# Order of the recurrence's level work and the weight splits in one segment of a transformer kernel

## The reference

```python
u = rmsnorm(h, attn_norm_w)
q, f_raw, i_in, g_out, b_gate, c_gate, x_conv, gate_a, gate_b = split(u @ w_in)
q = silu(q); f = lb + (1 - lb) * sigmoid(f_raw); logf = log(f); k = 1 - f; v = i_in
# per head, in chunks, G = cumsum(logf):
A[t, s] = sum(q[t] * k[s] * exp(G[t] - G[s]))   for s <= t
o = (q * exp(G)) @ S + A @ v                     # S: state from the chunks before
y_b = b_gate * causal_dwconv(c_gate * x_conv, conv_w)      # three taps
merged = sigmoid(gate_a) * rmsnorm(o) * silu(g_out) + sigmoid(gate_b) * y_b
```

## Time and profile before

| | |
|---|---|
| median of 3 runs | 1200.52 us (1199.38 to 1200.52) |
| the profiled execution | 1200.52 us, its span 1198.7 us |
| TensorE busy | 1149.8 us, 96% |
| VectorE busy | 878.9 us, 73% |
| ScalarE busy | 616.6 us, 51% |
| "conv" on TensorE | 784.4 to 883.9 us |

### The profile page before, as it was taken

How to read it: one execution, slowest core, us unless ns; L and a number is a source line. 1 busy time by engine, 2 the same in 40 slices (tenths; PEclk the granted TensorE clock), 3 DMA queues, 4 the chain that set the end, 5 groups by cost and what they waited for, 6 DMA issues and landing times.

```text
span 1198.7 us, 22749 instructions
## 1 busy us (share of the span) xinstructions
PE 1149.8 (96%) x8630; PEld 1088.2 (91%) x8630; DVE 878.9 (73%) x1486; ACT 616.6 (51%) x989; POOL 70.6 (6%) x134
## 2 busy tenths in 40 slices
PE   4999989999999999899999999999999999999997
PEld 4898679999888898799998889999999999999997
DVE  5799788998887985696554577787764766777643
ACT  4547546444336566654443465544443646555532
POOL 0101110211111310000000000000000000000000
PEclk9899989999999999999999999999999999999999
DMA  9947656999874743476455334433333453555531
GB/s 365 413 167 264 237 202 221 367 394 356 291 300 141 248 157 120 155 281 219 175 179 206 141 121 148 156 139 107 141 141 106 164 187 111 207 180 192 188 141 36
DMA packets 43131, 241.67 MB, mean 202 GB/s; under 512 B 5152, under 2 KB 7584, under 8 KB 20400
## 3 DMA queue, kind: packets, MB, share of 16 engines
q1 hardware_dynamic: 28912, 191.29, 44.3%
q0 software_dynamic: 14144, 49.37, 11.6%
HBM read 237.48 MB, written 1.06 MB: 199 GB/s over the span
## 4 chain that ended last, share of the span: by engine, by line
PE 82%; DVE 8%; ACT 5%; issue 3%; DMA 1%; SPq 0%; POOL 0%; DVEq 0%; ACTq 0%; POOLq 0%
PE acc L1914 20%; PE acc L1915 19%; PE acc L1916 19%; PE aux L2024 3%; PE aux L2026 3%; PE aux L2025 3%; PE aux L2401 2%; DVE wlo L1043 2%; ACT whi L583 1%; DMA x<-xT 1%; PE aux L1916 1%; PE aux L1914 1%; PE aux L1915 1%; ACT free_hlo L628 1%; PE aux L2055 1%
## 5 line engine op out<-in xcount | busy, mean ns | idle before, releaser
L1914 PE MATMUL acc<-hhi,whi 128*128 128x256 f32 (+3 forms) x1976 | 567.2, 287 | 6.8 <-DVE hlo L1064 4.0
L1915 PE MATMUL acc<-hlo,whi 128*128 128x256 f32 (+3 forms) x1976 | 560.2, 283 | 0.0
L1916 PE MATMUL acc<-hhi,wlo 128*128 128x256 f32 (+3 forms) x1976 | 557.7, 282 | 0.0
L1043 DVE TENSOR_TENSOR wlo<-raw,whi 128x1024 fp32r<-128x1024 f32 x338 | 412.8, 1223 | 178.6 <-ACT whi L583 178.1
L583 ACT ACTIVATE whi<-raw 128x1024 fp32r<-128x1024 f32 x338 | 357.1, 1057 | 189.7 <-PE acc L1916 119.4
L1914 PEld LDWEIGHTS acc<-hhi,whi 128*128 128x128 f32 x1976 | 374.0, 189 | 12.0 <-DVE hlo L1064 6.2
L1916 PEld LDWEIGHTS acc<-hhi,wlo 128*128 128x128 f32 x1976 | 375.7, 190 | 0.0
L1915 PEld LDWEIGHTS acc<-hlo,whi 128*128 128x128 f32 x1976 | 374.5, 190 | 0.2
L1072 DVE CUSTOM_DVE_ANT_0 lev<-lev,vec 128x1024 f32<-128x1024 f32 x56 | 71.7, 1280 | 1.9 <-DMA lev<-side_weights 1.9
L2026 PE MATMUL aux<-wlo,ahi 128*128 128x512 f32 x176 | 69.5, 395 | 0.0
L2024 PE MATMUL aux<-whi,ahi 128*128 128x512 f32 x176 | 69.4, 394 | 0.0
(11 more groups left out here) (372 smaller groups left out, 1518.0 us busy)
## 6 DMA issues: line engine op xcount, KB each, us to landing
raw<-weights SPq DMA_DIRECT2D x171, 1024.0 KB, 4.8
lev<-side_weights POOLq DMA_DIRECT2D x76, 512.0 KB, 6.0
qkv<-weights SPq DMA_DIRECT2D x3, 1024.0 KB, 14.6
x<-ln_rows POOLq DMA_DIRECT2D x6, 512.0 KB, 6.6
lev<-weights SPq DMA_DIRECT2D x2, 1024.0 KB, 20.1
big<-side_weights POOLq DMA_DIRECT2D x4, 512.0 KB, 5.7
big<-qkv POOLq DMA_DIRECT2D x32, 64.0 KB, 2.5
x<-gate_rows POOLq DMA_DIRECT2D x3, 512.0 KB, 6.9
```

The lines of the kernel that those rows point to most:

```text
L1043: v.tensor_tensor(wlo[:, m % SPLIT, :], raw_unit(i, m), whi[:, m % SPLIT, :].bitcast(F32), ALU.subtract).then_inc(lo_ready, 1)
L1914: mm(o, whi[:, u % SPLIT, w], hi, start=start, stop=False, skip_group_check=True)
L1915: mm(o, whi[:, u % SPLIT, w], lo, start=False, stop=False, skip_group_check=True)
L1916: return mm(o, wlo[:, u % SPLIT, w], hi, start=False, stop=stop_, skip_group_check=True)
```

## The change

On VectorE the two steps of `conv_first` go from ahead of the weight split to behind it and behind the unit's convolution work, in `conv_unit`. `read_pairs` stays behind them. On ScalarE `decay` goes from the head of `conv_unit` to behind the copy into `side` and the copy of the values. No instruction is added or taken away, and TensorE's and the queues' lists stay as they were.

```diff
@@ ScalarE
             def conv_unit(i, j):
                 k, r = divmod(j, 3)
                 bank = acc[(a0c + j) % 4]
-                if j in (2, 6, 10, 14):
-                    decay(3 + j // 4)
                 if r == 0:
                     unit_done(act, i, m0c + j)
...
                     A(side[:, k % 2, 0:T4], bank[:, 0:T4], ACT.Copy).then_inc(acc_free[(a0c + j) % 4], 1)
                 if j in VALUES_AT:
                     value_tokens(VALUES_AT.index(j))
+                if j in (2, 6, 10, 14):
+                    decay(3 + j // 4)
@@ VectorE
-            def conv_first(j):
-
-                if j in (0, 4, 8, 12, 16):
-                    level_scale(2 + j // 4)
-                if j in (1, 5, 9, 13):
-                    distances(3 + j // 4)
-
             def conv_unit(i, j):
...
                     v.tensor_tensor(YB[:, k, 0:T3], conv[:, k % 2, 0:T3], bank[:, 0:T3], ALU.mult)\
                         .then_inc(acc_free[b], 1)
+                if j in (0, 4, 8, 12, 16):
+                    level_scale(2 + j // 4)
+                if j in (1, 5, 9, 13):
+                    distances(3 + j // 4)
                 if j in (2, 6, 10, 14, 18):
                     read_pairs(2 + j // 4)
...
-            segment("conv", conv_unit, head=24, first=conv_first)
+            segment("conv", conv_unit, head=24)
```

## The result

The changed kernel takes 1210.93 us (1208.62 to 1214.31, 4 runs) against 1199.99 us, a ratio of 1.0093 with a 95% interval of 1.0072 to 1.0114: slower, 10.9 us, where 4.0 us were forecast and the range ended at 1206.0. The profiled execution took 1210.17 us, its span 1208.4 us, 9.7 us over before.

A forecast was written before the change was run, and what follows sets the result against it. TensorE, busy 96% of the span, was taken to set the time. Waits of 1.66, 1.50 and 1.67 us less 0.86 given back summed to 3.97 us over 1200.52, so 1204.5 us; range 1202.1 to 1206.0.

The forecast's parts named there:

- rival 3: TensorE's granted clock falls in the new waits at the level products: 1208.8 to 1212.0 us; chance 0.05.
- The splits first: Weight splits ahead of level work on VectorE: no gain from waits for `wlo`, put at 0, and cost 0.
- Level 2: Unit 0: `level_scale` done at 789.65, wanted at 790.51; cost 0, bound 0 to 0.3 us.
- Level 3: Unit 4: `level_scale` behind the convolution releases TensorE at 808.05, wanted at 806.39; wait 1.66 us.
- Level 4: Unit 8: delayed `decay(4)` on ScalarE and later VectorE work make TensorE wait 1.50 us.
- my low end: Level 4's wait without ScalarE's part, convolution held only by unit 7: about 0.25 us.
- Level 5: Unit 12: only a split of 1.14 us goes ahead of `level_scale(5)`, several us in hand; cost 0.
- Level 6: Unit 16: TensorE waits 1.67 us for `level_scale`; 0.86 us given back as the later transpose's wait goes.
- The sum: Waits at levels 3, 4 and 6 less what is given back: 3.97 us, 1204.5 us in all.
- The drain rule: Next VectorE operation starts only once the pipe is empty: each wait about 0.2 us longer, sum 4.6; not adopted.
- Rival 1: On ScalarE the later `decay(4)` delays nobody, leaving level 4's low end: 1203.2 us; chance 0.12.
- Rival 2: Level products stay in time, `level_scale(3)` done by 806.39; not slower, down to 1199.1 us; chance 0.15.

The follow-up runs named there:

- the filled kernel: Changed kernel with three constant 256-column products on TensorE in front of its waits at levels 3, 4 and 6; 1203.72 us, 1.0042.
- VectorE's part alone: Changed kernel with ScalarE's list put back, so decay stands at the head of the unit again; 1205.82 us, 1.0054.
- one filler: Changed kernel with one constant 256-column product on TensorE in front of each wait at levels 3, 4 and 6; 1209.54 us, 1.0074.
- unit 16 alone late: Changed kernel with level_scale back at the head in all units but unit 16; 1205.76 us, 1.0054.

## Why the prediction was right in its waits and wrong in its sum

**The step that failed** is the clock, which the sum puts at nothing and which cost 6.09 us. It was rival 3, "the clock falls in the new waits", and was given 0.05 on the ground that waits of up to 1.5 us in the first block had left the clock at 1.00 and that the new ones "stand in a stretch of dense matmuls". That stretch is dense, but the work right behind these waits is not: it is the level's 64-column products. And the longest wait between 130 and 150, 1.46 us, had products of up to 512 columns behind it. The runs show that the clock's 6 us go with these waits (the filled kernel), and that at level 6 it is the products right behind that matter: with wide ones put between, the clock held in every run. Behind the wait at level 3 it held even so, and what decides between that one and the others stays open. The rival's price, 1.45 to 2.5 us for each wait, was too low as well: a fall cost 3.03 and 3.06 us in the changed kernel's profile. Its count was too high, two falls there and not three. The two errors offset each other, so that the measured 1210.93 us lies within the rival's 1208.8 to 1212.0 by luck in part.

**The splits first, gain 0.** Right: no wait for `wlo` appears or goes.

**Level 2, cost 0.** Right.

**Level 3, 1.66 us.** Measured 1.62.

**Level 4, 1.50 us.** Measured 1.54. That ScalarE's delayed decay makes most of this wait is shown by VectorE's part alone, where 0.22 us of it is left; my low end was 0.25.

**Level 5, cost 0.** Right. The wait of 0.53 us ahead of it at 838.95 was there before (0.52 at 833.11).

**Level 6, 1.67 us, and 0.86 given back.** Measured 1.61, and the transpose no longer waits, as worked out.

**The sum, 3.97 us.** The lateness measured 3.91 us. The filled kernel shows it without the clock: from level 1's products to the transpose of the decayed keys its profile is 4.13 us longer than before, and its runs are 5.0 us over before, with an interval of 3.1 to 7.1.

**The drain rule.** `level_scale` starts at 822.75 and 823.96, 1.21 apart at a duration of 1.28, so the rows' spacing was the right term. The sentence of the Trainium skill ("VectorE: DVE Perf Modes", "The DRAIN you can't avoid") that I weighed is not all that the paragraph says: it adds that an operation that is not held starts earlier, and with that the trace does not disagree.

**Rival 1** (ScalarE's part costs nothing) fell: its part is free only while VectorE's list is as before. **Rival 2** (not slower) fell at the point named for it, unit 4.

## What to carry to other kernels

Before moving a step on a helper engine behind another one, look for a wait in the work it is moved behind: here the convolution's wait for the end of its own unit made a step of 2.4 us, with 3.6 us in hand, late by 1.6. Price a new wait of the tensor engine by the wait and by what the engine does right behind it: if narrow products follow, ask what half the clock would cost over the next several microseconds, since that can be more than the wait. If lateness can't be avoided, wide products ahead of the narrow ones, even useless ones, may cost less than the fall; and the small waits that are already there are found and removed the same way (reading the banks first gave 1.7 us).

## What the runs showed of the hardware

- A wait of 0.83 us, followed by narrow products, was followed by a granted clock of 0.53 from 827 to 834 (one filler); waits of 1.52 and 1.43 us, followed by products of 258 columns, were followed by 1.00; so was one of 1.47 us followed by 2.9 us of products of 256 columns and then the narrow ones.
- A stretch at the lower clock lasted some 6 to 10 us before full clock returned under the same products, and cost 3.0 to 3.1 us in the changed kernel's profile and 4.6 us in that with unit 16 alone late.
- The same wait does not always bring the fall: behind the wait at level 3 the clock held in all four profiles that have it, at 1.03 to 1.47 us with the same products behind, and the kernel with one filler ran from 1203.05 to 1211.11 us. These times go with the mean clock that each run lists, 0.991 for the fastest and 0.985 for the slowest. What decides between like waits stays open.
